# Two reorderings in a fused two-block kernel: the delta net's opening, and the mLSTM forget gate

## The reference, cut to what matters

```python
beta = jax.nn.sigmoid(b)
g = -jnp.exp(a_log) * jax.nn.softplus(a + dt_bias)
...
gc = jnp.cumsum(g, axis=-1)
kb = k * beta[..., None]
diff = gc[..., :, None] - gc[..., None, :]
decay = jnp.exp(jnp.where(causal_incl, diff, -jnp.inf))
lower = jnp.where(causal_strict, jnp.einsum('bhncd,bhnsd->bhncs', kb, k) * decay, 0.0)
tmat = lax.linalg.triangular_solve(eye + lower, eye, left_side=True, lower=True, unit_diagonal=True)
attn = jnp.einsum('bhncd,bhnsd->bhncs', q, k) * decay
```

```python
gates = proj[..., o2:o3] + b_gates          # 4 input gates, 4 forget gates
logf = jax.nn.log_sigmoid(f_pre)
b = jnp.cumsum(logf, axis=-1)
a = b_end[..., None] - b + ig
```

## Time and profile before

| | us |
|---|---|
| median of three runs | 1327.21 (1325.95 to 1331.6) |
| the profiled execution, its own time | 1326.52 |
| its span in the trace | 1324.7 |
| TensorE busy in it | 1281.9 (97%) |
| DVE, ACT, POOL busy | 590.6, 507.4, 564.0 |
| mean granted TensorE clock | 0.989 of full speed |
| share of TensorE in the chain that ended last | 86% |

### The profile page before, as it was taken

How to read it: one execution, slowest core, us unless ns; L and a number is a source line. 1 busy time by engine, 2 the same in 40 slices (tenths; PEclk the granted TensorE clock), 3 DMA queues, 4 the chain that set the end, 5 groups by cost and what they waited for, 6 DMA issues and landing times.

```text
span 1324.7 us, 15427 instructions
## 1 busy us (share of the span) xinstructions
PE 1281.9 (97%) x6025; PEld 1019.6 (77%) x6025; DVE 590.6 (45%) x844; ACT 507.4 (38%) x782; POOL 564.0 (43%) x426
## 2 busy tenths in 40 slices
PE   7989999999999999999999998999899999999997
PEld 5767887878888888888877765566688888888886
DVE  4987444351145211111486435665486414225124
ACT  5585325352222212212554435654364313223132
POOL 4334632545555544554553422211355444444440
PEclk9989999999999999999998999999899999999999
DMA  6422221323333333323332331101233333333311
GB/s 176 156 54 60 64 80 48 112 72 111 97 99 100 99 99 96 96 88 88 111 96 64 80 64 48 48 16 33 80 86 106 95 95 95 96 96 95 100 60 64
DMA packets 216304, 113.39 MB, mean 86 GB/s; under 512 B 21589, under 2 KB 214305, under 8 KB 215977
## 3 DMA queue, kind: packets, MB, share of 16 engines
q1 hardware_dynamic: 215128, 109.45, 29.1%
q10 hardware_dynamic: 976, 2.90, 0.6%
q0 software_dynamic: 128, 0.07, 0.0%
HBM read 110.03 MB, written 2.38 MB: 85 GB/s over the span
## 4 chain that ended last, share of the span: by engine, by line
PE 86%; DVE 4%; ACT 2%; issue 1%; POOL 1%; DVEq 0%; ACTq 0%
PE bank L1996 23%; PE bank L1998 23%; PE bank L1997 23%; PE bank L1137 1%; PE aux L2066 1%; PE aux L1077 1%; PE aux L1153 1%; PE bank L1015 1%; PE aux L1065 1%; PE bank L1017 1%; PE bank L1016 1%; PE bank L2044 1%; PE aux L1996 1%; POOL wl L1956 1%; PE bank L2046 1%
## 5 line engine op out<-in xcount | busy, mean ns | idle before, releaser
L1956 POOL TENSOR_TENSOR wl<-raw,wh 128x512 fp32r<-128x512 f32 (+1 forms) x402 | 545.6, 1380 | 724.2 <-ACT wh L2374 724.1
L2374 ACT CAST wh<-raw 128x1024 fp32r<-128x1024 f32 (+1 forms) x201 | 208.2, 1038 | 378.9 <-PE bank L1998 360.8
L1996 PE MATMUL bank<-ah,wh 128*128 128x512 f32 x888 | 351.9, 396 | 0.4 <-DVE craw L2770 0.4
L1998 PE MATMUL bank<-al,wh 128*128 128x512 f32 x888 | 345.9, 390 | 0.0
L1997 PE MATMUL bank<-ah,wl 128*128 128x512 f32 x888 | 345.8, 389 | 0.0
L1996 PEld LDWEIGHTS bank<-ah,wh 128*128 128x128 f32 x888 | 166.7, 188 | 40.2 <-issue 5.7
L1997 PEld LDWEIGHTS bank<-ah,wl 128*128 128x128 f32 x888 | 166.8, 188 | 34.8 <-issue 1.2
L1998 PEld LDWEIGHTS bank<-al,wh 128*128 128x128 f32 x888 | 166.7, 188 | 34.9
L1996 PE MATMUL bank<-yh,wh 128*128 128x512 f32 x488 | 190.6, 391 | 0.1
L1998 PE MATMUL bank<-yl,wh 128*128 128x512 f32 x488 | 190.0, 389 | 0.0
L1997 PE MATMUL bank<-yh,wl 128*128 128x512 f32 x488 | 189.9, 389 | 0.0
(11 more groups left out here) (451 smaller groups left out, 1545.1 us busy)
## 6 DMA issues: line engine op xcount, KB each, us to landing
raw<-in_w_up SPq DMA_DIRECT2D x54, 512.0 KB, 3.9
raw<-in_w_down SPq DMA_DIRECT2D x48, 512.0 KB, 3.9
raw<-in_w_in SPq DMA_DIRECT2D x39, 512.0 KB, 3.9
raw<-in_w_gate SPq DMA_DIRECT2D x22, 512.0 KB, 3.8
raw<-in_w_out SPq DMA_DIRECT2D x16, 512.0 KB, 3.7
raw<-in_ple_gate SPq DMA_DIRECT2D x8, 512.0 KB, 3.8
raw<-in_w_down SPq DMA_DIRECT2D x8, 384.0 KB, 3.3
xtok<-in_x SPq DMA_DIRECT2D x4, 512.0 KB, 5.1
```

What stands on the lines that cost most here:

```text
L1956: nc.gpsimd.tensor_tensor(wl[pl.slot[b]][:, half], raw[b % RAW][:, half], wh[pl.slot[b]][:, half].bitcast(F32), ALU.subtract).then_inc(wl_ ...
L1996: nc.tensor.matmul(ps, h[:, c:c + P], mh[:, k, :], start=(n == 0), stop=False)
L1998: last = nc.tensor.matmul(ps, h[:, c:c + P], ml[:, k, :], start=False, stop=(n == nk - 1))
L2374: nc.scalar.copy(wh[pl.slot[b]][:, 0:w], raw[b % RAW][:, 0:w]).then_inc(wh_ready, 1)
```

## The change

Delta net. The subtraction with clamp moves from VectorE to ScalarE, as Relu with scale -1 and a bias, and the Exp takes the sign back. ScalarE runs it, and the small factors `eg`, behind `head_norm(0)` and a weight rounding. TensorE runs all four grams behind tile v 1, each in an `aux` of its own, and the key transposes behind v 2, into four `aux`. VectorE goes norms, then beta, mask chunk by chunk, then all `decayed`, then `kd`, conv 8, conv 9, then `solve`, and only then the queries' norms and conv 10 and 11. `h32` has three buffers in the norms. SP sends the blocks out behind the load of tile ch 0 instead of cc 0. ScalarE's second `head_norm` moves behind `conv_evac(11)`.

Gates. The weight columns are loaded twice with a shift of four, so that the forget gates stand at partitions 32 to 35, and `bs` is written to partitions 0 to 3. The three selecting matmuls, `nbs` and two semaphores go; `c4` is one subtraction on VectorE behind conv 1. On ScalarE `conv_silu(1)` and `conv_silu(2)` move between the reads of the v2 tiles. The bias is loaded by two DMAs instead of one.

```diff
-                return [(d[:, :, 0:64], w[:, :, 1536:1600]), (d[:, :, 64:96], w[:, :, end - 32:end]),
+                return [(d[:, :, 0:32], w[:, :, 1536:1568]), (d[:, :, 32:64], w[:, :, 1540:1572]),
+                        (d[:, :, 64:96], w[:, :, end - 32:end]),
...
-        DIAG_OUT, DIAG_BACK = pl.tiles[pl.at["cc", 0]][2], pl.tiles[pl.at["cc", 1]][2]
+        DIAG_OUT, DIAG_BACK = pl.tiles[pl.at["ch", 0]][2], pl.tiles[pl.at["cc", 1]][2]
...
-            pe.wait_ge(forget_sums_ready, 1)
-            nc.tensor.matmul(aux[0][0:H, :], ident[0:8, 0:H], g2[:, :], start=True, stop=False)
-            nc.tensor.matmul(aux[0][0:H, :], ident[0:8, H:2 * H], nbs[:, :], start=False, stop=True)
-            nc.tensor.matmul(aux[1][0:H, :], ident[0:8, H:2 * H], bs[:, :], start=True, stop=True).then_inc(cb_ps, 1)
...
             conv_evac(2)
-            conv_silu(1)
-            conv_silu(2)
             for pair in range(2):
                 if pair == 1:
                     conv_evac(3)
                 for c in range(NC):
+                    if pair == 0 and c in (1, 3):
+                        conv_silu((c + 1) // 2)
...
-            nc.vector.tensor_scalar(nbs[:, :], bs[:, :], -1.0, None, ALU.mult).then_inc(forget_sums_ready, 1)
...
+            scaled_qk(1)
+            conv(0)
             dve.wait_ge(ncol_ps, 1)
             nc.vector.tensor_copy(ncol[:, :], aux[3][:, 0:NC]).then_inc(ncol_ready, 1)
-            scaled_qk(1)
-            conv(0)
             scaled_qk(2)
-            dve.wait_ge(cb_ps, 1)
-            nc.vector.tensor_copy(c4[:, :], aux[0][0:H, :]).then_inc(c4_ready, 1)
+            conv(1)
+            nc.vector.tensor_tensor(c4[:, :], g2[0:H, :], bs[:, :], ALU.subtract).then_inc(c4_ready, 1)
...
-            conv(1)
             conv(2)
...
                     if j >= H:
                         pe.wait_ge(head_rn, j - H + 1)
-                        pe.wait_ge(u_done, BETA_SCALED[j - H])
+                        pe.wait_ge(kd_ready, j - H + 1)
...
+            pe.wait_ge(head_normed, H)
+            pe.wait_ge(head_rn, H)
+            for c in range(NC):
+                gram(auxh[c], c, kT, gram_ps)
             gemm("v", 2)
-            pe.wait_ge(kd_ready, H)
-            gram(auxh[2], 2, kT, gram_ps)
-            gram(auxh[3], 3, kT, gram_ps)
+            for h in range(H):
+                pe.wait_ge(u_done, BETA_SCALED[h])
+                transpose4(aux[h], kT[:, h, :]).then_inc(kt_ps, 1)
             gemm("v", 3)
             head_sums(H)
...
-                    if j >= 2:
-                        act.wait_ge(head_normed, j - 1)
+                    if j >= 3:
+                        act.wait_ge(head_normed, j - 2)
...
-            decay_factors()
             head_norm(0)
+            split(pl.at["v", 0])
+            act.wait_ge(eg_args, 1)
             for c in range(NC):
-                act.wait_ge(dt_args, c + 1)
-                nc.scalar.activation(AT[:, c], AT[:, c], ACT.Exp).then_inc(dt_exp, 1)
+                for h in range(H):
+                    i = nc.scalar.activation(AT[:, c, h, :], GR[:, h, c * P:(c + 1) * P], ACT.Relu,
+                                             bias=gT[:, c, h:h + 1], scale=-1.0)
+                link(i)
+                nc.scalar.activation(AT[:, c], AT[:, c], ACT.Exp, scale=-1.0).then_inc(dt_exp, 1)
+            decay_factors()
+            split(pl.at["v", 1])
...
-            for c in range(NC):
-                for h in range(H):
-                    i = nc.vector.tensor_scalar(AT[:, c, h, :], GR[:, h, c * P:(c + 1) * P], gT[:, c, h:h + 1], 0.0,
-                                                ALU.subtract, ALU.min)
-                i.then_inc(dt_args, 1)
...
-            conv(11)
-            solve()
+            solve()
+            for j in range(H, 2 * H):
+                head_norm(j)
+            conv(10)
+            conv(11)
```

More of the change, by code:

```diff
@@ L372, in build @@
         late = offs["kf"] + 1024
-        g2 = sb("g2", [2 * H, T], at=late)
-        lf = sb("lf", [2 * H, T], at=late + 2048)
-        bs = sb("bs", [2 * H, T], at=late + 4096)
-        nbs = sb("nbs", [2 * H, T], at=late + 6144)
+        g2 = sb("g2", [32 + H, T], at=late)
+        lf = sb("lf", [32 + H, T], at=late + 2048)
+        bs = sb("bs", [H, T], at=late + 4096)
         c4 = sb("c4", [H, T], at=late + 8192)
@@ L2565, in _ @@
             conv_evac(11)
+            tables(LN_EXP_TABLES)
+            head_norm(H)
+            split(pl.at["hp", 0])
             conv_silu(10)
@@ L2900, in _ @@
             link(i)
-            decayed(0)
-            decayed(1)
-            beta_scaled(2)
-            beta_scaled(3)
-            decayed(2)
-            decayed(3)
+            for c in range(NC):
+                decayed(c)
+            dve.wait_ge(eg_exps, 1)
+            link(nc.vector.tensor_tensor(eg[:, 0, :, :], eg[:, 0, :, :], gT[:, :, 12:16], ALU.mult))
+            for h in range(H):
+                dve.wait_ge(kt_ps, h + 1)
+                nc.vector.tensor_tensor(kd[:, :, h, :], auxh[h][:, :, :], over_chunks(eg[:, 1, :, h]),
+                                        ALU.mult).then_inc(kd_ready, 1)
+            conv(8)
             conv(9)
-            for j in range(H, 2 * H):
-                head_norm(j)
             def scaled_v(h):
```

70 lines of the change are left out of this document (25 added, 45 removed).

## The result

The changed kernel takes 1319.72 us (median of seven runs, 1317.56 to 1322.04); the kernel before, on the same chip, 1326.57 (1325.68 to 1332.2). The ratio is 0.9932, 95% interval 0.9914 to 0.995. The forecast was 1318.4, range 1314.5 to 1322.5. The profiled execution took 1320.03 us, its span is 1318.2 (1324.7 before): 6.5 us less.

The account below looks back on a forecast made before the run. TensorE, busy 97% of the span, was taken as the bound, so only its waits, work or clock count. From 1326.52 us, 4.4 (delta net, 6.2 - 1.8) and 3.7 (gates) came off: 1318.4, range 1314.5 to 1322.5.

Parts of the forecast that it names:

- (a): Delta net, gap before the grams: TensorE goes on 4.3 us earlier, key transposes at full clock; together 6.2 us.
- (b): Delta net, behind the grams: clamps on ScalarE at 0.30 us each cause no new TensorE wait at the key transposes.
- (c): Delta net: queries' norms behind the solver on VectorE make TensorE wait at the value transposes; cost 1.8 us.
- (d): Gates: without three selecting matmuls v2 starts 3.3 us earlier, slow matmuls gain 1.7 more; pair 0 ends 5.0 earlier.
- (e): Gates, v2 pair 1: late conv 2 delays SiLU, read and rounding; TensorE waits 2.35 us, gain shrinks from 5.0 to 3.7.
- R2: Rival: the clock falls in the new waits of 1.5 and 2.35 us; 1320.2 for one, 1322.0 for both; chance 0.29.
- R3: Rival: ScalarE switches tables between Relu and Exp in the delta net, seven loads; slower, 1330 to 1335; chance 0.04.

Follow-up runs that it names:

- its repeat: The kernel after, unchanged, run once more beside three other kernels: 1320.2 us, ratio 0.9939 to the kernel before.
- table loads: The kernel after with the activation table loaded anew between the groups of four clamps and the Exp, 7 loads in all: 1328.97 us, ratio 1.0003.
- SiLU late: The kernel after with ScalarE's third SiLU moved behind the read of the last v2 tile of pair 0: 1316.69 us, ratio 0.9914.
- gates alone: The kernel before with only the gates' part of the change, the delta net's opening as it was: 1324.91 us, ratio 0.9969.
- solver late: The kernel after with VectorE's solver put back behind the queries' norms and conv 10 and 11: 1324.71 us, ratio 0.9969.
- clamps on VectorE: The kernel after with the decay clamps back on VectorE, ahead of conv 6 and 7: 1322.33 us, ratio 0.9971.
- two buffers: The kernel after with two buffers instead of three for ScalarE's norms: 1319.36 us, ratio 0.9927.
- the neighbouring kernel: The kernel after with the third SiLU behind the read and the first query norm inside the solver, no filling matmuls: 1321.78 us, ratio 0.9942.

## Why the prediction was right, step by step

The forecast was 1.3 us low and within its range. The terms:

- **(a), the gap: 4.3 us plus 1.9 of clock.** The wait is 0.96 us instead of 5.55 (forecast 1.2), and the transposes behind v 2 run at full clock. Counted from the first sums of squares TensorE had earned 6.4 us when it got to the value transposes; the step had 6.2. Right, and the run with the clamps put back shows that they made 3.7 of the 4.6 us. The third buffer, to which the step gave the fourth norm's freedom, was not needed for that.
- **(b), no new wait.** Right: the four chunks are ready at 83.8, 85.6, 87.5 and 89.3 us (forecast 83.7, 85.5, 87.4, 89.2); a Relu costs 0.32 us (0.30), and no table load stands between. TensorE has no wait at the key transposes.
- **(c), the solver in VectorE's queue: 1.8 us.** The chain was right: load landed at 102.0 (102.3), solver done at 111.25 (111.8), two of its instructions stretched by 1.0 us each. The memset cost nothing, as the sum had it. The Trainium skill (SBUF — State Buffer, "SBUF: two separate sides") has it so, and the trace agrees: beside the memset the solver's instructions take 0.22 to 0.23 us. The size was off: the wait was 0.76 us where I had 1.5, and with 0.1 behind it the cost was 0.9 us, half of the 1.8. Block one gained 5.1 us up to `Y`, 5.5 without the later start, 4.4 by the forecast. One sentence of this step fell: "its result buys nothing". With the solver left late the transposes of `Y` waited 3.6 us. The solver began 3.3 us earlier there than in the kernel before (114.76 against 118.02) and still ended 0.9 us later: GpSimd's halves, which before began at 125.52, just behind it, came at 121.00 and met it.
- **(d), the gates' start.** v2 starts 3.48 us sooner relative to the small matmuls (3.3), at full clock.
- **(e), pair 1.** The mechanism was exact (conv 2, SiLU, read, rounding, GpSimd); conv 2 ended 0.7 us sooner than forecast, so the wait is 1.66 us and not 2.35, and the gain 4.44 us instead of 3.7, before the clock. Moving the SiLU brought pair 1 0.83 us forward.
- **R2, the clock falls in the new waits (0.29).** It did in one of the two, in pair 1: 1.49 us in the kernel after and its repeat, and none with the wait at 0.85 or filled. I had 1.7 to 1.9 for one. The wait of 0.76 us had no fall. So part of R2 came true inside the forecast, and its time for one fall, 1320.2, is nearer to the measured one than the forecast is.
- **What no step had** is the fall behind the third head, 1.79 us in a stretch that the change does not touch. The forecast took unchanged stretches as unchanged.

In all, 0.7 and 0.7 us better than forecast in block one and at the gates, 0.24 more behind `Y`, then 1.49 and 1.79 of clock: 1318.4 - 1.7 + 3.3 = 1320.0, and the profiled run took 1320.03. The mechanisms were right; that the time was so near is luck, because errors of both signs met. R3's mechanism is not in the kernel after, as forecast, and its price was too high: the run with table loads has the time of the kernel before (ratio 1.0003), where R3 had 3.5 to 8.5 us more. The solver's end, 121.00, was as R3 had it; the wait of 10 us ahead of the value transposes was not there.

## What to carry to other kernels

When a chain moves up, look at what stays in place beside it and at what moves onto it: the solver, left where it was, lost its slack to GpSimd's halves. Before swapping two steps on one engine, follow what is queued behind them, since the rounding behind a norm decides where GpSimd meets VectorE. And price a half clock only where TensorE is the one that is waited for. Before two profiles are compared by start times, take off what they differ by ahead of the change.

## What the hardware showed that I had not expected

**The same wait, a fall or none.** The wait of 3.35 us in the third head stands unfilled in thirteen of the fourteen profiles (before, after and the twelve runs) and was followed by half clock in eleven. The stretch behind it lasts 134.6 us in the two without a fall (before, SiLU late), 134.8 where it was filled, and 136.1 to 139.0 with a fall. The wait ahead of pair 1, 1.65 to 1.70 us, cost 1.49 us in five profiles (after, its repeat, gates alone, solver late, clamps on VectorE) and nothing in two (two buffers, table loads), with the same rows around it. The Trainium skill (TensorE: Matmul & The Clock Gate, "What's actually happening") says that the activity monitor is free-running and does not start with the kernel. These profiles fit that, since equal waits at different moments were caught or not; that the moment alone decides is not shown by a run. Executions of one kernel differ in the same way: many of the kernel before lie near 1326.5 us with a granted clock of 0.989, and many near 1331 with 0.984. So an unchanged stretch can differ here by 1.5 to 4.4 us from one profile to the next, and the 1.79 us above need not be the change's.

**Fillers help only where something is idle and TensorE is waited for.** 13 matmuls in the right wait saved 2.7 us against the neighbouring kernel, though in one profile only, and two of thirteen unfilled ones had no fall either. In the wrong place they cost 2.96 us. At the second MLP 18 kept the clock at full speed, where each of the other thirteen profiles has half clock, and saved nothing.
